# Order of the opening work: row conversions before squares, a low part made by VectorE, the sum of squares inside the third slab

## What is computed

```
h = x * rsqrt(mean(x * x, -1) + EPS) * norm_g
z = h @ w_in
(c_glu, c_gate, r_q, r_k, r_v, ...) = split(z)
v = a * sigmoid(b)            # a, b = halves of c_glu
y = conv31(v) + db            # depthwise, 31 taps
q, k = rotary(r_q), rotary(r_k)
```

## Time and profile before

| | |
|---|---|
| median of 3 runs | 2974.97 us (2973.96 to 2975.1) |
| profiled execution, its own time | 2974.12 us |
| its span | 2972.3 us |
| TensorE busy | 2943.6 us, 99% |
| VectorE, ScalarE, GpSimd busy | 64%, 43%, 48% |

### The profile page before, as it was taken

How to read it: one execution, slowest core, us unless ns; L and a number is a source line. 1 busy time by engine, 2 the same in 40 slices (tenths; PEclk the granted TensorE clock), 3 DMA queues, 4 the chain that set the end, 5 groups by cost and what they waited for, 6 DMA issues and landing times.

```text
span 2972.3 us, 43739 instructions
## 1 busy us (share of the span) xinstructions
PE 2943.6 (99%) x15008; PEld 2456.6 (83%) x15008; DVE 1894.3 (64%) x2852; ACT 1283.1 (43%) x2068; POOL 1438.3 (48%) x1056
## 2 busy tenths in 40 slices
PE   8999999999999999999999999999999999999998
PEld 6888888878888888888887888888888888798997
DVE  7985677874524598577697634367772353784756
ACT  4233333484332423333347633246563323553634
POOL 5443443455555444443355545543444444555745
PEclk9999999999999999999999999999999999999999
DMA  4322322213333332222221233332223323323322
GB/s 153 99 72 77 92 78 83 88 43 100 92 99 102 121 99 80 91 83 73 79 92 58 78 95 104 92 121 71 78 71 100 103 81 120 100 100 100 108 92 86
DMA packets 73870, 271.34 MB, mean 91 GB/s; under 512 B 8192, under 2 KB 9088, under 8 KB 73088
## 3 DMA queue, kind: packets, MB, share of 16 engines
q1 hardware_dynamic: 70560, 254.84, 27.7%
q10 hardware_dynamic: 3168, 14.61, 1.4%
HBM read 264.17 MB, written 5.24 MB: 91 GB/s over the span
## 4 chain that ended last, share of the span: by engine, by line
PE 84%; issue 7%; POOL 5%; DVE 2%; ACT 1%; DVEq 0%; POOLq 0%; ACTq 0%
PE gem L576 15%; PE gem L578 15%; PE gem L577 15%; POOL wlo L473 5%; PE xp L1151 2%; PE gem L1011 2%; PE xp L1153 2%; PE xp L1152 2%; PE gem L1013 2%; PE gem L1012 2%; PE gem L701 2%; PE gem L703 2%; PE gem L702 2%; PE gem L821 2%; PE gem L823 1%
## 5 line engine op out<-in xcount | busy, mean ns | idle before, releaser
L473 POOL TENSOR_TENSOR wlo<-raw,whi 128x512 fp32r<-128x512 f32 x820 | 1134.9, 1406 | 1357.4 <-ACT whi L1236 1357.4
L1236 ACT ACTIVATE whi<-raw 128x1024 fp32r<-128x1024 f32 x410 | 432.3, 1056 | 492.3 <-PE gem L578 335.9
L576 PE MATMUL gem<-zhi,whi 128*128 128x512 f32 x1312 | 512.1, 390 | 0.3 <-DVE zlo L2012 0.3
L578 PE MATMUL gem<-zhi,wlo 128*128 128x512 f32 x1312 | 510.7, 389 | 0.0
L577 PE MATMUL gem<-zlo,whi 128*128 128x512 f32 x1312 | 510.5, 389 | 0.0
L576 PE MATMUL gem<-hhi,whi 128*128 128x512 f32 x1104 | 430.2, 390 | 0.0
L578 PE MATMUL gem<-hhi,wlo 128*128 128x512 f32 x1104 | 429.6, 389 | 0.0
L577 PE MATMUL gem<-hlo,whi 128*128 128x512 f32 x1104 | 429.5, 389 | 0.0
L576 PEld LDWEIGHTS gem<-zhi,whi 128*128 128x128 f32 x1312 | 246.4, 188 | 51.7 <-DVE zlo L2012 0.8
L578 PEld LDWEIGHTS gem<-zhi,wlo 128*128 128x128 f32 x1312 | 246.3, 188 | 51.6
L577 PEld LDWEIGHTS gem<-zlo,whi 128*128 128x128 f32 x1312 | 246.4, 188 | 50.7
(11 more groups left out here) (511 smaller groups left out, 6016.2 us busy)
## 6 DMA issues: line engine op xcount, KB each, us to landing
raw<-in_slabs SPq DMA_DIRECT2D x446, 512.0 KB, 3.5
U<-in_slabs SPq DMA_DIRECT2D x32, 512.0 KB, 3.8
U<-in_x SPq DMA_DIRECT2D x4, 512.0 KB, 6.7
U<-in_x ACTq DMA_DIRECT2D x1, 2048.0 KB, 9.4
xsave<-U ACTq DMA_DIRECT2D x1, 2048.0 KB, 6.7
U<-xsave ACTq DMA_DIRECT2D x1, 2048.0 KB, 9.3
out_y<-yr SPq DMA_DIRECT2D x8, 256.0 KB, 2.2
tab<-in_tab_ret ACTq DMA_DIRECT2D x2, 512.0 KB, 5.2
```

Source lines behind the costliest of these rows:

```text
L473: part = pool.tensor_tensor(wlo[:, k % 4, c], raw[:, k % 2, c], whi[:, k % 4, c].bitcast(f32), O.subtract)
L576: pe.matmul(o, wh, hi, start=(n == 0), stop=False)
L578: mm = pe.matmul(o, wl, hi, start=False, stop=(n == len(terms) - 1))
L1236: act.activation(whi[:, k % 4, :], raw[:, k % 2, :], A.Copy).then_inc(hi_done, 1)
```

## The change

ScalarE converts all eight rows and the second slab first, then makes the eight squares, with the high part of the third slab after the second square; the high part of the fourth slab moves from `layer` to here, ahead of the five constant loads. VectorE splits all rows, then makes the low part of the second slab (in two halves) in GpSimd's place, and then adds the squares. GpSimd makes slab 0's low part, waits for VectorE's, and goes on with the third. TensorE takes all rows of slab 0, all of slab 1, three of slab 2, then the sum of squares, then the rest.

```
@@ gpsimd
-            at = 0
+            low(0, 0)
+            pool.wait_ge(lo_done, 2)
+            at = 2
@@ tensor
-                    plain_rows(0, 0, 5, arriving=True)
-                    plain_rows(1, 0, 5)
+                    plain_rows(0, 0, NT, arriving=True)
+                    plain_rows(1, 0, NT)
+                    plain_rows(2, 0, 3)
                     square_sum(L, 0)
-                    plain_rows(0, 5, NT, arriving=True)
-                    plain_rows(1, 5, NT)
-                    plain_rows(2, 0, NT)
+                    plain_rows(2, 3, NT)
@@ scalar
-                square(0, i, XN[:, i, :])
                 if i == 0:
                     act.wait_ge(vec_in, 16)
                 plain_high(0, i)
-                if i == 4:
-                    high(0, 1, False)
-            high(0, 2, False)
+            high(0, 1, False)
+            for i in range(NT):
+                square(0, i, XN[:, i, :])
+                if i == 1:
+                    high(0, 2, False)
+            high(0, 3)
@@ scalar, layer
-                high(g0 + GLU[0], 3)
+                if L:
+                    high(g0 + GLU[0], 3)
@@ vector
-                if 0 < i < 7:
-                    add_square(0, i)
                 plain_split(0, i)
+
+            dve.wait_ge(hi_done, 2)
+            dve.wait_ge(lo_done, 1)
+            for c in (slice(0, T), slice(T, 2 * T)):
+                low_second = tt(wlo[:, 1, c], raw[:, 1, c], whi[:, 1, c].bitcast(f32), O.subtract)
+            low_second.then_inc(lo_done, 1)
+            for i in range(1, 7):
+                add_square(0, i)
```

## The result

The changed kernel takes 2979.13 us (median of 20 runs, 2978.52 to 2979.88) against 2974.99 us (2973.82 to 2976.83) before: 4.1 us or 0.14% more, ratio 1.0015 with a 95% interval of 1.0009 to 1.002. It is slower, by less than the 0.2% that was set as the mark: its fastest run lies 1.7 us above the slowest of the kernel before. The forecast was +3.6 us.

What follows compares the result with a forecast made beforehand. Two chains bound 20 to 128 us: TensorE's matmuls, and VectorE's from the sum of squares. The sum 3.8 us later makes the values' third bank 3.6 us later: 2974.97 + 3.6 = 2978.6 us, range 2975.4 to 2980.2.

Steps and rivals of the forecast that it cites:

- VectorE's chain from the sum of squares to the values: From 20 to 128 us: a chain nearly without slack, 3.8 us later, making the values' third bank 3.6 us later.
- no wait at the values: Stated sign of being wrong: TensorE not waiting for VectorE's rotary products, where waits at about 125 and 129 were expected.
- The slack of 0.2 us at the third bank: At the values: third bank released at 126.51, used by TensorE at 126.72 before the change.
- The start: First rows: VectorE's split held back by GpSimd's work until 8.08, TensorE beginning at 9.0, no earlier than before.
- The sum: Sum of squares on TensorE: behind 57 slab matmuls instead of 30, starting at 24.0 instead of 20.23, 3.8 us later.
- The fifth slab: TensorE 2.4 us ahead, waits 1.0 for the low part, starts near 35.6, waits on normed rows, ends about 43.6.
- The +1.2: Leaving the fifth slab: TensorE 1.2 us later than before because of the last normed row.
- From there both engines are shifted alike: Behind the values: no pause gives the 3.6 us delay back.
- Late adds: Rival, opening: all six adds contended, ending at 25.0, sum 1 us later still; +4.6, 2979.6 us; chance 0.11.
- slack in the chain: Rival, convolution chain: hidden slack, so only the normed rows stop TensorE; +1.2 us, 2976.2; chance 0.12.
- normed rows that stay hidden: Rival, fifth slab: normed rows cost nothing and filled holes stay won; -2.4 us, 2972.6; chance 0.10.
- The clock's rival: Before the sum: matmuls stay at 0.43 us well beyond 13.4, each microsecond costing 0.47, up to +11; chance 0.04.

Runs made afterwards that it cites:

- e1: Changed kernel with the sum of squares on TensorE right behind slab 1, not behind three rows of slab 2; 2976.30 us.
- e4: e1 with six taps of the first channel tile of layer 0's convolution left out, shortening VectorE's chain; 2974.07 us.
- e11: Changed kernel with 11 filler matmuls before the fifth slab's seventh row, in a free bank of slab products, VectorE's program unchanged; 2979.14 us.
- e2: Kernel before with only the sum of squares moved, behind slabs 0 and 1 and three rows of slab 2; 2980.30 us.
- e7: Kernel before with its TensorE order, VectorE making slab 1's low part, and five rows' conversions ahead of squares and adds; 2973.82 us.
- e14: The changed kernel measured again, unaltered; 2979.07 us.
- e8: e7 with slab 1's high part before the fourth square and slab 3's high part between the second and third normed row; 2972.22 us.
- e12: Changed kernel with one more VectorE instruction, an already satisfied wait, ahead of the first convolution tap; 2977.63 us.
- e6: Kernel before with only slab 1's low part moved from GpSimd to VectorE, behind the fifth row's split; 2972.94 us.
- e9: Changed kernel with 11 filler matmuls before the fifth slab's seventh row, in a bank that VectorE's first tap must wait for; 2977.57 us.
- e13: e8 with one more wait for VectorE; 2972.84 us.
- e10: e9 with six taps of the first channel tile of layer 0's convolution left out; 2975.59 us.

## Why the prediction was right

**The bound.** That VectorE's chain from the sum of squares to the values sets the end was the main step, and e1, e4 and e11 show it. The changed kernel's own trace hardly does: the prediction named "no wait at the values" as a sign of being wrong, and there the engine idles for 0.13 us and takes one step of 0.52 us instead of 0.23. The slack of 0.2 us at the third bank (logarithm less third bank) measured 0.14 to 0.18 us in e1, e2, e7, e11, e14 and the changed kernel.

**The start.** No gain there was forecast, since the first split would stand beside GpSimd's work, and it began no earlier: 8.80 instead of 8.86. But the row doesn't test the reason, since the first conversion itself came at 6.97 in this execution, not at 6.51. e1 does, where the first conversion is at 6.54:

```profile
7.41 5.93 DVE L2121 SCALAR_TENSOR_TENSOR zlo<-U,vec,zhi 128x512 fp32r<-128x512 f32 x8 [7.41 <-ACT zhi L1295]
```

VectorE's eight splits take 5.93 us instead of 5.39, the first of them 1.30 instead of 0.75, and TensorE starts at 8.92. GpSimd's low part runs to 8.15, so the half microsecond was indeed taken away.

**The sum.** Forecast 24.0, measured 23.74: the matmuls went to the 0.23 us pace at 13.0, not 13.4. How near this came is in part luck: five more executions with the same opening began the sum between 23.21 and 24.42, mostly by when the clock rose. The low part of slab 1 was done at 14.43 (14.9). The third slab's low part met two of the adds, the adds' end at 21.15 was before the forecast 21.7, and neither counted.

**The fifth slab.** The loss in it was right: start at 35.38 (forecast 35.6), the next slab at 44.15 (43.6). The stop is at the seventh row, not the eighth: VectorE's pause of 0.5 us, before the fourth slab's product in the old kernel, now lies between the last two normed rows and delays both low parts. The +1.2 measured +1.3. Missed is the fall of the clock behind the wait, 1.8 us more, so that TensorE came to the values 3.1 us late and not 1.2, and lost 0.3 us there and not 2.4. The forecast doesn't feel it: both ways lead to the same third bank, forecast +3.6, measured +3.4. That is luck too: with another 0.3 us of low clock, TensorE's own delay would have set the end, by a term that the prediction put at nothing.

**Behind the values.** "From there both engines are shifted alike" was nearly right: +3.38 at the values, +3.54 at 1503 us. Then come 0.36 us from the pause of VectorE near 1520 us. That makes 3.9 of the medians' 4.1 us, with 0.5 us from pauses and steps that no part of the forecast names; the rest is within what the two values round which the runs lie leave open.

**The rivals.** Late adds, slack in the chain, and normed rows that stay hidden are refuted by the rows above. The clock's rival named the wrong place: the clock rose early, but fell once more later.

## What to carry to other kernels

Filling the holes of the busiest engine gains only if the small serial work that others hang on isn't pushed back for it: here TensorE was 2.6 us ahead of before at the end of the fourth slab, bought with 3.5 us on the sum of squares, and those were paid in full 100 us later, where nothing of the edit is to be seen. Before moving such a step, follow its consumers engine by engine to the next place where the busiest engine takes their result, and set the delay against the slack there, at each such place. If both chains are at their limit, move both, in the same edit (e8). And before comparing two traces, read where the chain starts in each: here the logarithm moved by 0.9 us between e14 and e11, whose openings are the same.

## What the runs showed of the hardware

- A standstill of 2.6 us at the fifth slab was followed by 3 us of matmuls at 0.43 us (granted clock 0.78 in 42.3 to 50 us), and one of 2.1 us there in e2 as well (0.57 in 46 to 50); one of 1.7 us at the same place in e1 was not (1.00 from 40 to 50), nor the one of the changed kernel filled with matmuls in e11. The two kernels in which it fell had also stood still for 0.8 to 0.9 us some 5 us before, e1 had not, and no run separates the two. In e2 a wait of 1.5 us before 15.55, soon after the first rise, was followed by matmuls at 0.43 us until 19 (granted clock 0.50 from 15.8 to 19.2); one of 1.28 us before 15.52 in the kernel before was not. So the length of a standstill alone doesn't tell whether the clock falls.
- The first rise of the clock did not come at the same time in every execution. With the same opening and a start at 8.8 to 8.9 us, the last matmul step of 0.43 us began at 11.5 us in e12, 12.0 in e14, 12.35 in the changed kernel's trace and 13.7 in e11; the sum of squares began at 23.39, 23.52, 23.74 and 24.42.
- Between 2600 and 2650 us TensorE waits 4.5 us in four pieces in both kernels. In the changed kernel's execution a stretch at the low clock follows (0.89 from 2635 to 2650), in that of before none (1.00). It cost 1.5 us (+3.87 to +5.35), about 0.5 of which came back by 2676, and the stretch was there in the traces of e2, e4, e6, e9, e11, e12, e13 and e14, not of e1, e7, e8 and e10. Runs of before lie round two values 1.2 us apart, and this is probably why. The upper ones have the lower mean clock (0.998 against 0.999), and where a kernel's runs fall apart by it, the traced execution is at the upper value with the stretch (e6, e13) and at the lower without it (before, e8, e10). No run was made to test it.
- One more instruction in VectorE's program removed pauses of 0.4 and 0.5 us that the profile puts down to issue, as far as 1400 us behind it (e12 against e14, e13 against e8). Why is open. Differences of up to 0.8 us between kernels whose programs differ in length can be that alone.
